# Making the low parts of the weights in pieces of 1024 columns every fourth slot, in a hybrid decoder step

## The reference

```
x += RMSNorm_post( W_out [ mLSTM heads | retention heads | gated-DeltaNet heads ]( W_in RMSNorm_pre(x) ) )
x += RMSNorm_post( squared-ReLU MLP( RMSNorm_pre(x) ) )
```

## Time and profile before

| | us |
|---|---|
| median of 3 runs | 3311.73 (3311.37 to 3312.37) |
| the profiled execution | 3308.99 |
| its span, first to last instruction | 3307.3 |
| PE busy | 3127.6 (95%), 23264 matmuls |
| VectorE busy | 1987.9 (60%), of it 1084.5 in 1668 low parts (L1126) |
| ScalarE busy | 1423.1 (43%) |
| GpSimd busy | 171.0 (5%) |
| mean granted TensorE clock | 0.985 of full speed |

### The profile page before, as it was taken

The page is one execution under the profiler, slowest core; times in us unless marked ns, Lnnn a source line. Parts: engine busy times, 40 slices in busy tenths (PEclk is TensorE's granted clock), DMA queues, the critical chain, the costliest instruction groups (busy, mean ns, idle before and its releaser), DMA issues.

```text
span 3307.3 us, 72069 instructions
## 1 busy us (share of the span) xinstructions
PE 3127.6 (95%) x23264; PEld 3062.7 (93%) x23264; DVE 1987.9 (60%) x4003; ACT 1423.1 (43%) x3148; POOL 171.0 (5%) x225
## 2 busy tenths in 40 slices
PE   5999999999999999999969999999989999999997
PEld 5888898998999999999958989999989999999997
DVE  5777765666555545455567777566665455454555
ACT  4555543344433434334345555334444333343333
POOL 0111111110000000000011111111000000000000
PEclk9999999999999999999979999999999999999998
DMA  3334444553454444444424344545435545444444
GB/s 133 126 129 131 132 154 156 167 160 127 156 169 160 167 161 165 165 165 166 153 72 132 124 133 135 162 153 183 152 115 170 167 160 168 161 165 165 165 165 147
DMA packets 266059, 499.23 MB, mean 151 GB/s; under 512 B 34272, under 2 KB 39552, under 8 KB 265664
## 3 DMA queue, kind: packets, MB, share of 16 engines
q1 hardware_dynamic: 243360, 443.56, 40.9%
q0 software_dynamic: 14496, 51.05, 4.6%
q10 hardware_dynamic: 8064, 2.80, 0.3%
HBM read 475.30 MB, written 22.01 MB: 150 GB/s over the span
## 4 chain that ended last, share of the span: by engine, by line
PE 76%; DVE 12%; issue 5%; ACT 3%; DMA 2%; DVEq 1%; ACTq 0%; SPq 0%; POOLq 0%; POOL 0%
PE PU L461 68%; PE PABCD L461 4%; DVE WL L1126 2%; PE PE_ L461 2%; DMA RAW<-in_w 2%; PE PF L461 2%; ACT WH L793 1%; ACT AE L793 1%; DVE Y L1140 1%; DVE Y L1291 1%; DVE PMS L1410 1%; PE PABCD L464 1%; DVE AE L1482 1%; DVE X L1143 0%; DVE Y L1316 0%
## 5 line engine op out<-in xcount | busy, mean ns | idle before, releaser
L461 PE MATMUL PU<-HH,WH 128*128 128x288 f32 x4096 | 1284.8, 314 | 59.1 <-DVE HL L1131 47.8
L793 ACT ACTIVATE WH<-RAW 128x512 fp32r<-128x512 f32 x1669 | 964.6, 621 | 635.5 <-PE PU L461 462.8
L461 PE MATMUL PU<-HL,WH 128*128 128x288 f32 x4096 | 1212.5, 296 | 0.0
L461 PE MATMUL PU<-HH,WL 128*128 128x288 f32 x4096 | 1208.5, 295 | 0.0
L1126 DVE TENSOR_TENSOR WL<-RAW,WH 128x512 fp32r<-128x512 f32 x1668 | 1084.5, 694 | 184.7 <-ACT WH L793 172.3
L461 PEld LDWEIGHTS PU<-HH,WH 128*128 128x128 f32 x4096 | 774.7, 189 | 79.0 <-DVE HL L1131 49.2
L461 PEld LDWEIGHTS PU<-HL,WH 128*128 128x128 f32 x4096 | 776.2, 190 | 7.1
L461 PEld LDWEIGHTS PU<-HH,WL 128*128 128x128 f32 x4096 | 775.0, 189 | 0.0
L461 PE MATMUL PU<-UH,WH 128*128 128x288 f32 x2560 | 759.0, 296 | 3.2 <-DVE UL L1280 2.0
L461 PE MATMUL PU<-UL,WH 128*128 128x288 f32 x2560 | 755.2, 295 | 0.0
L461 PE MATMUL PU<-UH,WL 128*128 128x288 f32 x2560 | 752.7, 294 | 0.0
(11 more groups left out here) (245 smaller groups left out, 2279.9 us busy)
## 6 DMA issues: line engine op xcount, KB each, us to landing
RAW<-in_w SPq DMA_DIRECT2D x1669, 256.0 KB, 3.8
SIN<-in_sin POOLq DMA_DIRECT2D x32, 512.0 KB, 4.3
out_sout<-Y POOLq DMA_DIRECT2D x32, 512.0 KB, 5.4
BC<-gate_rows POOLq DMA_DIRECT2D x32, 304.0 KB, 4.1
AUX<-in_aux POOLq DMA_DIRECT2D x32, 152.0 KB, 3.5
X<-in_x SPq DMA_DIRECT2D x4, 576.0 KB, 7.6
out_y<-X SPq DMA_DIRECT2D x4, 576.0 KB, 2.8
Y<-in_gw POOLq DMA_DIRECT2D x2, 1024.0 KB, 5.1
```

What stands on the lines that cost most here:

```text
L461: return nc.tensor.matmul(out, lhsT, rhs, start=start, stop=stop, skip_group_check=True)
L793: return nc.scalar.activation(out, in_, f, **kw)
```

## The change

RAW becomes one tensor, of which RAW[0] to RAW[3] are views, so that one instruction can read two chunks that lie side by side. VectorE's `lo_part` of one chunk is replaced by `lo_pair` of two: it waits for the high part of the second chunk as well, subtracts 1024 columns, and counts `lo_ready` up by two. It stands in the slots 3, 7, 11, ..., 31 (t % 4 == 3), each time for the chunks 2m and 2m+1 with m = t // 4 + 2. The odd chunk keeps the slot that it had. The even chunk moves two slots later. The programs of the other engines are as they were.

```diff
-        RAW = [sb(f"RAW{i}", [128, NC_ // 4, HD]) for i in range(4)]
+        RAWS = sb("RAW", [128, NC_, HD])
+        RAW = [RAWS[:, 4 * i:4 * i + 4] for i in range(4)]
...
-            def lo_part(Q, p, joined=None):
-                s, c = divmod(p, 4)
+            def lo_pair(Q, m, joined=None):
+                s, half = divmod(m, 2)
                 if joined is not None and s in (2, 3):
-                    if c == 0:
+                    if half == 0:
                         dve.wait_ge(sem("three_quarters_done"), 2 * joined + s - 1)
-                    if c == 3:
+                    else:
                         dve.wait_ge(sem("unit_done"), 4 * Q + s + 1)
-                elif c == 0:
+                elif half == 0:
                     dve.wait_ge(sem("unit_done"), 4 * Q + s + 1)
-                dve.wait_ge(sem("hi_ready"), 16 * Q + p + 1)
-                k = slice(4 * c, 4 * c + 4)
-                tt(WL[s % 2][:, k], RAW[c][:], WH[s % 2][:, k].bitcast(F32), ALU.subtract).then_inc(sem("lo_ready"), 1)
+                dve.wait_ge(sem("hi_ready"), 16 * Q + 2 * m + 2)
+                k = slice(8 * half, 8 * half + 8)
+                tt(WL[s % 2][:, k], RAWS[:, k], WH[s % 2][:, k].bitcast(F32), ALU.subtract).then_inc(sem("lo_ready"), 2)
...
-                    if t % 2:
-                        lo_part(Q, t // 2 + 4, l if last_head else None)
+                    if t % 4 == 3:
+                        lo_pair(Q, t // 4 + 2, l if last_head else None)
...
-            for p in range(4):
-                lo_part(0, p)
+            for m in range(2):
+                lo_pair(0, m)
```

More of the change, by code:

```diff
@@ L335, in load @@
                 src = d["w"][unit, :, k] if isinstance(unit, int) else d["w"][bass.ds(unit, 1), :, k].rearrange("a p k m -> p (a k) m")
-                sp.dma_start(RAW[c][:], src).then_inc(sem(f"raw_in{c}"), 16)
+                sp.dma_start(RAW[c], src).then_inc(sem(f"raw_in{c}"), 16)
             for c in range(4):
@@ L807, in hi_part @@
                 k = slice(4 * c, 4 * c + 4)
-                fn(WH[s % 2][:, k], RAW[c][:]).then_inc(sem("hi_ready"), 1)
+                fn(WH[s % 2][:, k], RAW[c]).then_inc(sem("hi_ready"), 1)
             def prenorm(l, e, gain):
```

## The result

The changed kernel takes 3406.67 us (median of 4 runs, 3402.14 to 3415.56), the kernel before 3312.05 in the same comparison (4 runs): a ratio of 1.0284, 95% interval 1.0266 to 1.0303. The change costs 2.8%. I had forecast 3353 and a range up to 3396: slower was right, the size was not, and the time lies 11 us above the range. The profiled execution spans 3401.0 us against 3307.3: 93.7 us to explain, where I had 42.

A forecast was written before the change was run, and what follows sets the result against it. PE was taken as the bound: its own work in the MLP, a few VectorE and ScalarE chains elsewhere. Terms 10 + 16 + 12 + 1 + 3 - 6 + 6 = +42 us on 3308.99, plus 2.7 to the median: 3353, range 3321 to 3396.

The forecast's parts named there:

- The instruction's price: VectorE: a 1024-column low part takes 1.22 us, saving 0.07 us a pair, 58 us of VectorE's time in all.
- the some 100 that I named as a sign: Sign that the forecast is right: in the profile after, VectorE is some 100 us less busy.
- Term 1, norms: Behind each norm PE waits for chunk 4, now tied to chunk 5: 2.8 us, 2.1 ahead of the MLP; +10 us.
- Term 2, mLSTM: Between mLSTM heads: late load +1.5 us, two pairs in the chain +0.53 each; six quads, +16 us (10 to 22).
- Term 3, retention: Six retention quads: late load and one pair ahead of step 1, 2.0 us each; +12 us (7 to 15).
- Term 4, DeltaNet: Sixteen DeltaNet quads: slot 13 without a low part helps, the head-end wait only moves; -6 us (-20 to +8).
- The gain that I named in slot 13: DeltaNet: without slot 13's low part the activation behind it starts 0.6 us earlier, and PE's wait of 0.5 goes.
- Term 5, the clock: Granted clock at half speed for 3 us behind a third of some 16 new PE waits; +6 us (0 to 20).
- rival A: MLP and W_out: loads bind, loops of 6.47 and 6.37 us against 6.40; +36 us (+22 to +50), 3389; chance 0.22.
- the MLP at 0: MLP: PE's own work alone counts as long as weights arrive, so no change, still 812 us.
- Rival B: DeltaNet: relief for VectorE wins, sixteen quads gain up to 1.6 us each, -26 us; 3296 in all; chance 0.06.

The follow-up runs named there:

- late_singles: Changed kernel's slots, but two 512-column low parts one behind the other, each with its own wait and buffer release: 3386.29 us (1.0207 to the kernel before).
- joint_small_pool: joint_release with GpSimd's state product cut to 128 of 1024 columns (7 of 8 samples' states left undecayed): 3324.92 us (1.0012).
- before_small_pool: Kernel before with GpSimd's state product cut to 128 of 1024 columns (7 of 8 samples' states left undecayed): 3273.57 us (0.9871).
- after_small_pool: Changed kernel with GpSimd's state product cut to 128 of 1024 columns (7 of 8 samples' states left undecayed): 3358.34 us (1.0126).
- pair_slot15: Kernel before with one pair alone: in DeltaNet quads chunks 10 and 11 get their low part together in slot 15, none in slot 13: 3313.48 us (0.9985).
- joint_release: Kernel before, low parts unchanged, but the even chunk's buffer is loaded again only when the odd one's low part is done: 3400.99 us (1.0256).

## Why the prediction was wrong

**The instruction's price** held (1.22 us forecast, 1.225 measured), but VectorE's busy time fell by 46 us (1987.9 to 1941.7), not by the some 100 that I named as a sign (my own sum had given 58): the low parts fell by 64.5 (1084.5 to 1020.0), other instructions grew by 18.

**Term 1, norms**: right. 5.6 and 4.2 us forecast, 5.4 and 4.0 measured apart from the clock, by the mechanism named (late_singles removes the wait of chunk 4 for chunk 5, and the term with it).

**Term 2, mLSTM**: the places were right, the size was not: +28.5 for the six quads, +25.1 apart from the clock, where I had 16 (10 to 22). The small-product kernels divide it, if the parts add:

| part, six mLSTM quads | from | us | forecast |
|---|---|---|---|
| late loads, no collision | joint_small_pool - before_small_pool | 17.1 | 9 |
| the rest of the change, no collision | 23.5 - 17.1 | 6.4 | 6.4 |
| the collision with GpSimd | 28.5 - 23.5 | 5.0 | 0 (0 to 4) |

(23.5 is after_small_pool - before_small_pool.) The failed step is "The load that ScalarE needs is the second of its burst [...] I take +1.5". I charged the late load once a quad, where it starts the head's chain. That place was about right: the gate's exponential stands 1.3 us later behind the sum. But late loads cost 2.9 us a quad by themselves; at which other instructions they do so was not separated. In after the waits stand at the pairs behind the chain: PE waits 11.7 us for WL in the three quads of the first layer, six waits of up to 2.2, and I had priced the pair only as a delay of the head's chain. The second miss is GpSimd's product, 0 to +0.7 and nothing in the sum, measured 0.8 a quad.

**Term 3, retention**: 7.3 apart from the clock, 13 forecast.

**Term 4, DeltaNet**: wrong sign, +6.3 apart from the clock instead of -6. The failed step is "the pairs of slots 27 and 31 replace four low parts of slots 27, 29, 31 and 1: VectorE reaches head_done about 0.5 later". In the mean of 14 quads the low part of slot 29 gave back 0.46 us, but the pair of slot 27 took 0.54 more and that of slot 31 0.53 more. Between them VectorE waits 1.0 us for ScalarE, before as after: two short low parts would use that wait, the pair can't, since it needs the later high part. Late_singles shows it: its first short part runs inside the wait, VectorE is done 3.63 us behind the quad's end, as before (3.61), and in after 4.75: 1.1 later, where I had 0.5. PE's wait for head_done went from 0.6 to 1.7 us (24.0 us in 14 waits, 8.0 before). The gain that I named in slot 13 was real: 0.6 us, and pair_slot15 harvests it.

**Term 5, the clock**: +31 where I had +6 (0 to 20), the largest single miss. I had let the clock fall only behind the 3 to 5 us waits of terms 1 to 3. It also fell behind DeltaNet's chains of two middling waits (1.7 and 0.5 us around 188), six times in the first layer's DeltaNet quads and four in the second's. Nor does the length of one wait decide it: in before two waits of PE of 2.54 us ended at 489.8 and 563.2, and what follows them is (clock third from the end)

```profile
490.20:493.60 3.40, 3.40 (x28) 3.35 (x27) 3.09 (x8) 2.34 (x6) 0.61 (x1) 1.00 0.50 158
563.50:566.90 3.40, 3.40 (x16) 3.22 (x15) 2.04 (x7) 2.75 (x8) 0.61 (x1) 0.50 0.49 143
```

**The MLP and rival A**: the failed term is the MLP at 0. Rival A's loop was the right one and its numbers nearly so (6.78 and 6.46 by its sum, 7.00 and 6.56 measured); what I couldn't say was how often it binds. It bound in some 15 of 62 quads, for 11.7 us, under the 22 to 50 of the rival: elsewhere the burst is broken up into two lone pairs, as I had argued against it. Why it enters and leaves the burst is open. That the total of 3407 lies near the rival's 3389 is no merit of it: 82 of the 94 us are elsewhere.

**Rival B** was refuted: the DeltaNet quads didn't shorten. The rule that spoke for it, from the Trainium skill (VectorE: DVE Perf Modes, The TRN2 errata), gives the durations rightly (691 and 1224 ns by it, 694 and 1225 in the traces), but nothing of the 132 us that it would save can be seen in the span.

The sum apart from the clock is 62 us, forecast 36: 9 more in mLSTM, 12 in DeltaNet, 12 in the MLP, 6 less in retention. What joint_release adds to this is where the heads' part starts: the loads released late, by themselves, cost 83 us, the change with everything else 88 to 95, so the parts overlap. Without the collision, late loads alone against the whole change are 3.2 against 13.7 us in DeltaNet, where the rest holds the merging at the head's end, 17.1 against 23.5 in mLSTM, 15.9 against 12.2 in retention and 10.1 against 4.8 in the last head's quad. In the last two the whole change costs less than one of its parts. So the division under term 2 is a reading and not a measurement of its parts.

## What to carry to other kernels

Merging two instructions ties two consumers and two buffers together: price first who waits for the half that now comes late, and when the buffer that it releases is loaded again; the saved overhead comes last. Two short instructions can use a wait that stands between what they need; merged, both lie behind it (DeltaNet's head end, 0.5 us of VectorE and 1.1 us of PE's wait a quad). And where an engine off the critical path can block another one (here GpSimd's 1.93 us), look at which instruction it falls on before and after: a shift of a microsecond moves the block from slack onto the chain, and moving it was worth 37 us here.

## What the runs showed of the hardware

- **A VectorE instruction can stand until GpSimd's has ended.** Beside GpSimd's 1.93 us product the gate's instruction (310 ns alone) took 1349, 2385 or 2402 ns, and each time it ended 0.18 us behind the product, whenever it had begun. The other direction exists too: in before, at 91.15, a low part that had begun 0.10 us ahead of the product made it 2.37 us long. Other VectorE instructions in the same stretch keep their time (AM, which reads PSUM, 344 ns). By the Trainium skill (SBUF — State Buffer, SBUF: two separate sides) the shared port pair is an exclusive lock against VectorE operations in a 2-port mode or with two SBUF inputs, whoever starts first gets it, and the other fully blocks. The trace agrees on the blocking, but not on who gets it: in joint_release the gate began 0.30 us ahead of the product by the profile and still ended behind it. That 1/8 of the product's columns takes 1.3% off the kernel is what I hadn't expected.
- **A 512 KB load landed in 3.6 us** beside 3.1 for the first of two 256 KB loads, 3.5 for the second, and 3.9 for a later one in a burst of four issued 0.6 us apart. One load of twice the size was out of the way sooner than the second of two. The Trainium skill (DMA: Bandwidth & Descriptors, Anatomy of one DMA) has for loads issued by GpSimd a fixed cost of about 2.0 us and bytes over 436 GB/s; worked out for 256 and 512 KB that is an estimate of 2.6 and 3.2 us. SyncE issues the loads here: the step of 0.6 agrees with the 0.5 measured, the level is 0.4 to 0.5 lower than the trace.
- **The MLP's loop has two patterns at one code** (bursts of four at 3.8 us, pairs at 3.5), each held for several quads, 26.4 us a quad in the one and 25.60 in the other.
